# Order of weight loads, conversions and transposes at the FFN phases of a two-layer GLA/Mamba-2 trunk

## The reference

```python
D_MODEL = 1024; SEQ = 256; DEPTH = 2; D_FF = 2816; MACARON_WEIGHT = 0.5
def swiglu(h, w_gate, w_up, w_down):
    return (jax.nn.silu(h @ w_gate) * (h @ w_up)) @ w_down
def reference(x, ...):
    for i in range(DEPTH):
        g = norm_gain[i]
        h = swiglu(rmsnorm(x, g[0]), ffn_w_gate[i, 0], ffn_w_up[i, 0], ffn_w_down[i, 0])
        x = x + MACARON_WEIGHT * rmsnorm(h, g[1])
        h = rmsnorm(x, g[2])
        ...
        h = gla_mixer(h, ...) or ssd_mixer(h, ...)
        x = x + rmsnorm(h, g[3])
        h = swiglu(rmsnorm(x, g[4]), ffn_w_gate[i, 1], ffn_w_up[i, 1], ffn_w_down[i, 1])
        x = x + MACARON_WEIGHT * rmsnorm(h, g[5])
    return x
```

## Time and profile before

| | |
|---|---|
| time, median of 3 runs | 1256.77 us (1255.92 to 1257.13) |
| the profiled execution: its own time | 1251.99 us |
| its span | 1250.2 us |
| TensorE (PE) busy | 1154.7 us, 92% |
| weight loads of TensorE (PEld) | 958.1 us, 77% |
| VectorE (DVE) busy | 767.0 us, 61% |
| ScalarE (ACT) busy | 601.3 us, 48% |
| GpSimd (POOL) busy | 50.9 us, 4% |
| moved by DMA | 195.04 MB, 156 GB/s over the span |

### The profile page before, as it was taken

The page is one execution under the profiler, slowest core; times in us unless marked ns, Lnnn a source line. Parts: engine busy times, 40 slices in busy tenths (PEclk is TensorE's granted clock), DMA queues, the critical chain, the costliest instruction groups (busy, mean ns, idle before and its releaser), DMA issues.

```text
span 1250.2 us, 17047 instructions
## 1 busy us (share of the span) xinstructions
PE 1154.7 (92%) x6189; PEld 958.1 (77%) x6189; DVE 767.0 (61%) x1230; ACT 601.3 (48%) x902; POOL 50.9 (4%) x73
## 2 busy tenths in 40 slices
PE   6899997799978999997999996999999978899998
PEld 5788886788766888886888885788888856688886
DVE  5555546465655455556555546889999885554553
ACT  6444444554454444455444445545455526444442
POOL 3000000000000000000000000211111110000000
PEclk9999998999988999999999997999999978899999
DMA  9655545164145655554555542254444404655540
GB/s 316 219 174 185 178 129 157 35 202 157 46 152 202 199 174 198 162 174 170 185 176 194 184 118 85 69 176 145 149 134 136 166 7 154 213 184 194 176 133 34
DMA packets 161678, 195.04 MB, mean 156 GB/s; under 512 B 6228, under 2 KB 145680, under 8 KB 161632
## 3 DMA queue, kind: packets, MB, share of 16 engines
q1 hardware_dynamic: 160288, 190.86, 47.1%
q0 software_dynamic: 1232, 3.52, 0.9%
q10 hardware_dynamic: 112, 0.05, 0.0%
HBM read 193.36 MB, written 1.05 MB: 156 GB/s over the span
## 4 chain that ended last, share of the span: by engine, by line
PE 80%; DVE 11%; ACT 4%; DMA 3%; issue 1%; SPq 0%; DVEq 0%; ACTq 0%
PE ps L1293 35%; PE ps L1312 23%; PE ps L1345 9%; PE ps L1355 6%; DMA raw<-in_ffn_w_up 3%; DVE ws L826 2%; DVE ws L908 2%; PE ps L1304 2%; ACT ws L488 1%; PE ps L1665 1%; PE ps L1641 1%; ACT ws L548 1%; DVE xT L898 1%; ACT xT L530 1%; PE ps L1459 1%
## 5 line engine op out<-in xcount | busy, mean ns | idle before, releaser
L1293 PE MATMUL ps<-ws,xT 128*128 128x512 f32 x2112 | 494.5, 393 | 11.9 <-DVE ws L908 11.9
L1293 PEld LDWEIGHTS ps<-ws,xT 128*128 128x128 f32 x2112 | 397.5, 189 | 99.6 <-DVE ws L908 14.6
L1312 PE MATMUL ps<-ws,hT 128*128 128x512 f32 x1344 | 351.7, 410 | 8.2 <-DVE hT L921 4.4
L1312 PEld LDWEIGHTS ps<-ws,hT 128*128 128x128 f32 x1344 | 255.1, 196 | 63.4 <-issue 11.5
L908 DVE TENSOR_TENSOR ws<-raw,ws 128x1024 fp32r<-128x1024 f32 x176 | 214.3, 1223 | 120.8 <-ACT ws L548 120.8
L826 DVE TENSOR_TENSOR ws<-raw,ws 128x2048 fp32r<-128x2048 f32 x92 | 210.7, 2292 | 118.0 <-ACT ws L488 118.0
L548 ACT ACTIVATE ws<-raw 128x1024 fp32r<-128x1024 f32 x176 | 184.8, 1058 | 154.9 <-PE ps L1293 138.0
L488 ACT ACTIVATE ws<-raw 128x2048 fp32r<-128x2048 f32 x92 | 174.8, 1913 | 48.4 <-PE ps L1312 45.5
L1345 PE MATMUL ps<-xT,ws 128*128 128x256 f32 x960 | 121.3, 287 | 4.3 <-DVE ws L826 4.1
L1345 PEld LDWEIGHTS ps<-xT,ws 128*128 128x128 f32 x960 | 118.6, 195 | 4.8 <-DVE ws L826 4.3
L1355 PEld LDWEIGHTS ps<-ws,xT 128*128 128x128 f32 x768 | 96.1, 197 | 12.6 <-DVE xT L898 6.7
(11 more groups left out here) (191 smaller groups left out, 627.9 us busy)
## 6 DMA issues: line engine op xcount, KB each, us to landing
raw<-in_ffn_w_down SPq DMA_DIRECT2D x88, 512.0 KB, 4.3
raw<-in_ffn_w_gate SPq DMA_DIRECT2D x86, 512.0 KB, 4.0
raw<-in_ffn_w_up SPq DMA_DIRECT2D x86, 512.0 KB, 5.0
raw<-in_ssd_w_in SPq DMA_DIRECT2D x48, 512.0 KB, 4.7
raw<-in_gla_w_in SPq DMA_DIRECT2D x24, 512.0 KB, 4.7
raw<-in_ssd_w_out SPq DMA_DIRECT2D x16, 512.0 KB, 4.4
raw<-in_gla_w_out SPq DMA_DIRECT2D x8, 512.0 KB, 5.3
gpost<-in_norm_gain POOLq DMA_DIRECT2D x6, 512.0 KB, 4.0
```

Source lines behind the costliest of these rows:

```text
L1293: mm = pe.matmul(ps[:, bank + t, :].rearrange("p (s n) -> p s n", s=2), xT[:, k, a, t * P:(t + 1) * P], ws[:, 0:2, b, k * UW:(k + 1) * UW] ...
L1312: mm = pe.matmul(ps[:, 2 * t + n, :], hT[:, par, j, a, t * P:(t + 1) * P], ws[:, slot, b, off:off + 512], start=(first and j + a + b == 0) ...
```

## The change

- SP: x tile 1 is no longer among the quarters; ACT issues its load right behind the one of the norm gains. In the first FFN phase the list becomes unit 1, down tile 0, unit 2, down tile 1, down tile 2, then down tile and unit from 3; in the other FFN phases down tiles 0 and 1, unit 1, unit 2, down tile 2, then as before.
- ACT and VectorE, first unit of a phase: quarters 0, 1 and 2 of unit 1, silus (in the first phase the silus come first), quarter 3, then down tile 0 and both hT. Second unit: down tile, quarters 0 and 1, silus, both hT, quarters 2 and 3. Loop bodies: quarter 3 comes behind both hT.
- ACT and VectorE at the start: both tiles of x, then the four quarters.
- FFN to mixer: one of the two input tiles is converted before the boundary, the other behind the last part of x inside it.
- TensorE: both pairs of transposes of a unit come together behind the down products of token tile 0. The sweep of unit 0 in the first phase goes k by k over both token tiles. `warm` multiplies zeros: five 512-column products ahead of the gain transpose, and five behind each x tile's transposes.

```diff
@@ SP @@
             for q in range(NQ):
                 quarter(ffn_w_gate[0, 0], 0, q)
                 quarter(ffn_w_up[0, 0], 1, q)
-                if q == 0:
-                    sp.dma_start(xres[:, 1, :], x[0, P:2 * P, :]).then_inc(x_in[1], 16)
...
-                    for u in range(2):
-                        load_down(wd, u * UW, *(a + b for a, b in zip(down_use(u), (0, n0[SLOT_DOWN[u]]))))
-                    for h in range(2):
-                        load_gate_up(wg, wu, 1, units + 1, h)
-                    for u in range(2, NF):
-                        load_down(wd, u * UW, *(a + b for a, b in zip(down_use(u), (0, n0[SLOT_DOWN[u % 2]]))))
...
+                    def load_unit(u):
                         for h in range(2):
                             load_gate_up(wg, wu, u, units + u, h)
+                    if ph > 0:
+                        load_down(0)
+                        load_down(1)
+                    load_unit(1)
+                    if ph == 0:
+                        load_down(0)
+                    load_unit(2)
+                    if ph == 0:
+                        load_down(1)
+                    load_down(2)
+                    for u in range(3, NF):
+                        load_down(u)
+                        load_unit(u)
...
@@ ACT (VectorE's list is changed in the same way, with lo, gate_up_lo, hidden and hT_low) @@
                     x_high(0, 0, range(KD))
-                    gate_up_hi(0, 0)
-                    gate_up_hi(0, 1)
                     x_high(0, 1, range(KD))
-                    gate_up_hi(0, 2)
-                    gate_up_hi(0, 3)
+                    for q in range(NQ):
+                        gate_up_hi(0, q)
...
                     x_high(b, 1, range(KD))
+                    first_hi(b, SLOT_P1 if slot == 0 else SLOT_P2)
                     return
...
+                def body(unit, down, par, early):
 
                     hi(*down)
-                    for q in range(2):
+                    for q in range(3 if early else 2):
                         gate_up_hi(unit + 1, q)
-                    if bank == A:
-                        gate_up_hi(unit + 1, 2)
                     for t in range(NT):
-                        gate(unit, t, bank)
-                    if bank != A:
-                        gate_up_hi(unit + 1, 2)
+                        gate(unit, t, A)
                     hT_high(unit, 0, par)
-                    gate_up_hi(unit + 1, 3)
                     hT_high(unit, 1, par)
-                body(0, units, (SLOT_DOWN[0], n0[SLOT_DOWN[0]]), 0, 0)
+                    for q in range(3 if early else 2, NQ):
+                        gate_up_hi(unit + 1, q)
+                if ph == 0:
+                    for t in range(NT):
+                        gate(units, t, 0)
+                for q in range(3):
+                    gate_up_hi(units + 1, q)
+                if ph > 0:
+                    for t in range(NT):
+                        gate(units, t, 0)
+                gate_up_hi(units + 1, 3)
+                hi(SLOT_DOWN[0], n0[SLOT_DOWN[0]])
+                for t in range(NT):
+                    hT_high(units, t, 0)
...
-                    first_hi(ph + 1, SLOT_P1)
-                    first_hi(ph + 1, SLOT_P2)
+                    first_hi(ph + 1, SLOT_P2 if PHASES[ph + 1][0] == "gla" else SLOT_P1)
...
             act.dma_start(grow, norm_gain.rearrange("l n (k c) -> (l n k) c", c=P)).then_inc(grow_in, 16)
+            act.dma_start(xres[:, 1, :], x[0, P:2 * P, :]).then_inc(x_in[1], 16)
...
@@ TensorE @@
                     for t in range(NT):
                         down_ready(unit - 1, t, slot, count)
-                        down_half(slot, par, t, 0, first)
-                        hidden_T(unit, t)
-                        down_half(slot, par, t, 1, first)
...
+                        for n in range(2):
+                            down_half(slot, par, t, n, first)
+                        if t == 0:
+                            hidden_T(unit, 0)
+                            hidden_T(unit, 1)
...
+                order = [(t, k) for t in range(NT) for k in range(KD)] if ph else [(t, k) for k in range(KD) for t in range(NT)]
+                for t, k in order:
...
+            def warm(count):
+
+                zeros = zr[:, :].rearrange("p (o n) -> p o n", o=1).broadcast_to([P, 4, P])
+                for _ in range(count):
+                    pe.matmul(ps[:, 0, :].rearrange("p (o n) -> p o n", o=4), zr[:, :], zeros, start=True, stop=True,
+                              skip_group_check=True)
+
+            pe.wait_ge(consts, CONST_IDENT + 1)
+            warm(5)
             pe.wait_ge(grow_in, 16)
             pe.transpose(ps[:, 3, 0:12 * KD], grow, ident[0:12 * KD, 0:12 * KD]).then_inc(gains_T, 1)
             for t in range(NT):
                 x_transposed(0, t)
+                warm(5)
```

More of the change, by code:

```diff
@@ L302, in load_gate_up @@
                     sp.dma_start(dst[:, ks, :], cols(w, col)[:, ks, :]).then_inc(gu_loaded[h], 16)
-            def load_down(wd, u, slot, count):
-                load_rows(slot, wd, u, None if isinstance(count, int) and count == 0 else count)
             def load_first(ph, slot):
@@ L961, in boundary @@
                     x_low(b, 1, range(KD))
+                    second = SLOT_P1 if slot == 0 else SLOT_P2
+                    lo(second, used_before(b, second))
                     return
@@ L1014, in ffn @@
                 elif ph + 1 < NPH:
-                    lo(SLOT_P1, used_before(ph + 1, SLOT_P1))
-                    lo(SLOT_P2, used_before(ph + 1, SLOT_P2))
+                    first = SLOT_P2 if PHASES[ph + 1][0] == "gla" else SLOT_P1
+                    lo(first, used_before(ph + 1, first))
             def gla_start(n0):
@@ L1422, in ffn @@
                     mm.then_inc(cols_T, 1)
-                sweep(units + 1, 1)
-                if ph == 0:
-                    pe.wait_ge(cols_done, 1)
-                for t in range(NT):
-                    down_ready(units, t, SLOT_DOWN[0], n0[SLOT_DOWN[0]])
-                    down_half(SLOT_DOWN[0], 0, t, 0, True)
-                    hidden_T(units + 1, t)
-                    down_half(SLOT_DOWN[0], 0, t, 1, True)
+                body(1, units + 1, SLOT_DOWN[0], n0[SLOT_DOWN[0]], 0, True)
                 with pe.Fori(1, NF // 2) as i:
@@ L1675, in mixer @@
                 pipeline(pe, n, body)
-            pe.wait_ge(consts, CONST_IDENT)
+            def warm(count):
[5 more added lines that the diff above has]
+            warm(5)
             pe.wait_ge(grow_in, 16)
```

72 lines of the change are left out of this document (40 added, 32 removed).

## The result

| | before | after |
|---|---|---|
| time, median | 1256.35 us (1253.31 to 1257.13, 4 runs) | 1225.88 us (1225.07 to 1226.76, 4 runs) |
| ratio after/before | | 0.9762, 95% interval 0.9744 to 0.978 |
| the profiled execution: time, span | 1251.99, 1250.2 | 1226.12, 1224.3 |
| TensorE busy | 1154.7, 92% | 1152.8, 94% |
| VectorE, ScalarE busy | 767.0, 601.3 | 763.9, 597.3 |

What follows compares the result with a forecast made beforehand. TensorE's own work was taken to bound the loops, with waits outside them. Terms 3.8 - 29.9 - 3.9 - 1.6 = -31.6 gave span 1218.6, time 1225 us; forecast 1219 to 1231 (chance 0.74), range 1217 to 1236.

Steps and rivals of the forecast that it cites:

- FFN starts: Starts of phases 3, 4 and 6: 17.6 us from end of sweep 0 to sweep 2, -29.9 for the three.
- The step behind it: Phases 3, 4 and 6: reordered quarters, down tiles and loads remove the 3.0 wait and the later one, within the -29.9.
- First phase: Start of the first FFN phase: sweep 2 near 53.7, not 49.84, behind down tile 1; +3.8, bounds 0 and +7.
- two of my signs: First phase: sweep 2 at 52 to 55, and a wait of 4 to 6 before the transposes.
- Rival (b): First phase: down tile 1 lands by 37 and the start loses nothing; 1221 us, chance 0.05.
- FFN to mixer: Two boundaries: one input tile converted ahead instead of two, -1.95 each, -3.9 together; bounds 0 and -3 each.
- Loops: 32 loop bodies: joining two pairs of transposes saves 0.05 us each, -1.6 together; bounds 0 and -3.
- Rival (c): Loop bodies: quarter 3 converted later makes the next load late and the sweep wait; 1290 us, chance 0.03.
- (a): Starts of phases 3, 4 and 6: the stall comes back behind VectorE; 1235 us, chance 0.12.
- (d): Starts of phases 3, 4 and 6: the 3.0 wait is for something else and stays; about 1240 us, chance 0.04.
- Zeros and x tile 1: Program start: fifteen zero products taken as 0; x tile 1 on ACT's queue gives issue time, no bandwidth gain counted.
- From span to time: Whole kernel: before's median lay 6.6 over its profiled span, so span 1218.6 was taken to time 1225.

Runs made afterwards that it cites:

- old conversions: The changed kernel with ACT's and VectorE's conversion order for the first two units of phases 3, 4 and 6 put back; median 1243.93 us.
- before again: The kernel before, unchanged, run and profiled a second time; median 1254.56 us, ratio 1.0004 to before.
- down tile 1 early: The changed kernel with down tile 1 loaded ahead of unit 2 in the first phase alone; median 1215.08 us.
- quarters first: The changed kernel with quarters 0 to 2 of unit 1 converted ahead of the silus in the first phase; median 1217.8 us.
- old loads: The changed kernel with SP's load order of phases 3, 4 and 6 put back, down tile 2 ahead of unit 2; median 1248.07 us.
- both repairs: The changed kernel with, in the first phase, down tile 1 loaded ahead of unit 2 and quarters 0 to 2 converted ahead of the silus; median 1209.69 us.

## Why the prediction was right, point by point

- **FFN starts, -29.9 forecast.** The traces give -10.07, -10.16 and -10.35, together -30.6. Sweep 0 of phase 3 ends 27 products into the row at 375.26 (these take 6.42 in the kernel with old conversions), so at 381.7, and sweep 2 starts at 399.08: 17.4 where I had 17.6. The walk through the queues held step by step. After's phase runs 7.97 later than before's (first conversion at 379.15, not 371.18). So my 388.0 for the second product with the up half becomes 396.0; it ended at 394.61 + 0.87 = 395.5. Down tile 1's high part, forecast 382.2, so 390.2, ended at 388.17 + 1.92 = 390.1. The wait of 0.3 that I booked didn't come. ScalarE in turn waited 0.68 for TensorE before its silus, so the loads of unit 2 held up nothing.
- **The step behind it** (the down tile and quarter order set both waits) held, and the runs with one order put back showed more than I had said: I booked the gain as one sum of conversions and loads, and neither has a part of its own. With either back, 24.5 and 25.2 of the 30.6 are lost, and 22.0 with both.
- **What I had not priced:** the merged pairs' cover in the starts. I gave them 0.05 a unit only. In the new order they bring 0.7 per start; with the old orders they are at most the 8.6 that stays, of which 5.2 is shorter waits. It belongs inside the -29.9, whose walk has all 12 products ahead of the transposes, so the sum didn't suffer.
- **First phase, +3.8 forecast, +5.9 between the two traces.** The mechanism was right: ScalarE stands at down tile 1, and the wait before the transposes is released in the end by its load. Of the size only this can be said: against before again it was +3.95, and the five traces with this list put sweep 2 at 52.62 to 56.51, so 3.8 and 5.9 lie in the same scatter. By after's trace alone two of my signs were missed by a little (52 to 55, and a wait of 4 to 6; it was 55.72 and 3.93). Step by step in that trace: the terms that I named for the first product add up to 14.3, not to the 14.7 that I wrote; it came at 13.57. Sweep 0 then took 12.78 in place of 10.9, at a granted clock of 0.65 in its first part (below), and ended at 26.35 for 25.6. The next step is the silus in front of unit 1. I had them done at 26.2; they were done at 27.90, as the table load of 1.28 began only at 25.76, with TensorE's release, where I took it for hidden. In the third phase of before it had run behind a quarter. So sweep 1 started at 30.15, not 28.5. I also booked no slow products there, and 24 of them took 7.35, not 5.74. As quarter 1 came later, so did the load that waits for it, and with it the tile: 43.1, not 40.9. TensorE, late itself by then, waited 3.93 in place of my 5.5, and the 12 slow products behind it cost 5.03 - 2.89 = 2.1, where I had 2. Of the errors 2.0 reached sweep 2, at 55.72 for 53.7; it lies inside my bounds of 0 to +7.
- **Rival (b), the start loses nothing,** is out for this kernel: the tile didn't land by 37. With the tile there in time it would have been near the truth: with down tile 1 early sweep 2 starts at 48.97, and with the quarters first as well at 43.83. Before had 49.84.
- **FFN to mixer, -3.9 forecast.** GLA -2.08 for -1.95. SSD -2.28 against before, -0.84 against before again, and +1.16 and +1.11 when put back; without the 24 small products at the end of the stage it is 2.07 in all four. Together 4.1, the term was right and a little too small. The wait of 2.19 went as forecast. My bound of -3 each, with the 12 products on the path, is out: their length changed nothing.
- **Loops, -1.6 forecast:** 0.047 a unit, -1.5.
- **Rival (c), the late quarter:** none of it. 11.04 a sweep and 16.82 a unit, with the fourth quarter behind both hT parts.
- **Rivals (a) and (d)** fall with the missing brackets in the third phase: no wait behind VectorE, and the wait before sweep 1 was for the quarter, as its row named it.
- **Zeros and x tile 1, 0 forecast:** 0.3 to 0.4 at sweep 0, and at sweep 2 nothing that can be told from the scatter. The Trainium skill, "DMA: Bandwidth & Descriptors", section "Rules for kernel authors", has it that a second queue brings issue time and no bandwidth. The runs are in line with it: SP issues its last quarter at 4.97 in after and at 5.42 with x tile 1 in its queue, the transposes of tile 1 start at 8.66 and 9.10, and the kernels take 1225.88 and 1225.48.
- **From span to time.** I carried 6.6 over from the span of before to its median. The right offset of after was 1.6 (1225.88 - 1224.3). That error of 5 to the high side was undone by one of the same size in the span: I had 1218.6, and it was 1224.3, of which 4.6 is the long GLA stage. The forecast of 1225 is so close to 1225.88 because the two are one thing: before was profiled in an execution with the short stage, and its usual one is the long one. Between the medians the change was -30.5, and the sum -31.6. The stages that the edits touch give -30.6 between the two traces. That the sum is within 1 of it is luck in part: first phase +2.1, FFN starts -0.7, mixers -0.5 (by the whole row) and loops +0.1 off the forecast, and the first of these alone scatters by more than that.

## What to carry to other kernels

Walk each in-order queue to the first instruction that waits, and ask what stands behind it that is wanted sooner: here a down tile a sweep too early on ScalarE and one load ahead of another on SyncE cost 10 us at each phase, and either alone brings 8 of them back. So two such edits are to be judged together; putting back one tells what it costs, not what it is worth alone. A wait of 3 to 4 us on TensorE cost from nothing to 2.9 more in the products behind it, so price a stall with them where TensorE sets the pace, and count a table load in front of an activation that waits as time on the path.

## What the runs showed of the hardware

- **The same instructions, two lengths.** The GLA stage, with short TensorE work between waits of 2 to 4 us, took 144.5 to 144.9 or 148.5 to 149.3 in nearly all traces, in the kernel before as well. The windows above tie it to the granted clock: 1.00 in one execution and 0.62 to 0.63 in another behind a wait of 2.25. What decides it in an execution stays open. Sweep 0 of the first phase shows the same: 48 products in 12.78 in after and 11.19 with the quarters first and with the old loads, though all start at 13.5 to 13.6 and the lists are the same up to there. Window of after:

```profile
13.50:16.00 2.50, 2.43 (x7) 1.95 (x8) 2.33 (x3) 1.87 (x2) 0.57 (x4) 0.65 0.54 103
```

Window of the kernel with the quarters first:

```profile
13.50:16.00 2.50, 2.41 (x11) 1.99 (x11) 2.20 (x3) 1.34 (x2) 0.60 (x4) 1.00 0.56 125
```

- **A table load can wait with its activation.** In after the load for silu began at 25.76, after 6.88 of idleness in which it could have run. In the kernel with both repairs it began at 24.93, right behind a quarter, when sweep 0 still had 1.5 to go. In the five traces with after's lists it came with the release each time, with the quarters first and with both repairs ahead of it. What puts it ahead of the wait in one list and behind it in the other was not tried.
